# Residual products with 1024 inputs: one matmul over both halves of the input in place of two, and a second add on VectorE

## The reference

```python
# first block, twice: mixer (a state space model, then stick-breaking attention), then SwiGLU
h = layer_norm(DEEPNORM_ALPHA * h + mix, ...)                       # mix = z @ w_out, o @ w_o     1024 inputs
h = layer_norm(DEEPNORM_ALPHA * h + swiglu_ffn(h, w_gu, w_down), ...)  # w_down: 2816 inputs
# second block, twice: attention and mLSTM side by side, then an MLP
x = x + mixed @ w_out                                               # 1024 inputs
u = relu(rmsnorm(x, norm_ffn) @ w_ff1)
x = x + (u * u) @ w_ff2                                             # 4096 inputs
```

## Time and profile before

| | |
|---|---|
| median of three runs | 1340.32 us (1340.19 to 1340.81) |
| the profiled execution's own time | 1339.62 us |
| its span | 1337.7 us |
| TensorE busy | 1312.3 us (98%), 10155 matmuls |
| VectorE busy | 961.5 us (72%), 1374 instructions |
| ScalarE busy | 693.6 us (52%), 872 instructions |
| hid_both matmuls of line 430 (512 columns) | 756, 394 ns each |
| hid_both matmuls of line 420 (256 columns) | 492, 280 ns each |
| reads from HBM | 169 GB/s over the span |

### The profile page before, as it was taken

One profiled execution on the slowest core, in us unless ns is written; L12 is line 12 of the kernel. 1 busy time (PEld: TensorE's weight loads), 2 busy tenths in 40 slices (PEclk: granted clock), 3 DMA queues, 4 the chain that ended last, 5 costly groups with the idle time before them and its releaser, 6 DMA issues.

```text
span 1337.7 us, 24857 instructions
## 1 busy us (share of the span) xinstructions
PE 1312.3 (98%) x10155; PEld 1221.3 (91%) x10155; DVE 961.5 (72%) x1374; ACT 693.6 (52%) x872; POOL 56.7 (4%) x31
## 2 busy tenths in 40 slices
PE   6899999999999999999999999999999999999999
PEld 4699998889999998889989999998898999999888
DVE  8966977757865987767897687775557867877542
ACT  5874654445765654444756644444445644544332
POOL 6910000000000000000000000000000000000000
PEclk9999999999999999999999999999999999999999
DMA  8676486666443586666454546567664545556762
GB/s 158 159 189 185 133 220 188 189 189 189 154 131 105 148 219 189 188 190 189 127 158 127 182 155 200 188 189 189 189 189 127 158 127 189 190 188 188 189 189 64
DMA packets 342810, 227.82 MB, mean 170 GB/s; under 512 B 22616, under 2 KB 337792, under 8 KB 342592
## 3 DMA queue, kind: packets, MB, share of 16 engines
q1 hardware_dynamic: 341200, 226.33, 59.2%
q10 hardware_dynamic: 1520, 0.20, 0.1%
HBM read 224.40 MB, written 1.05 MB: 169 GB/s over the span
## 4 chain that ended last, share of the span: by engine, by line
PE 88%; DVE 7%; ACT 3%; DMA 1%; issue 1%; POOL 1%; SPq 0%; DVEq 0%; ACTq 0%; POOLq 0%
PE PS L430 22%; PE PS L420 15%; PE PS L421 15%; PE PS L422 15%; PE PS L431 11%; DVE w_lo L401 2%; ACT w_hi L396 1%; PE PS L1419 1%; DMA toep<-toep 1%; DVE xn L1213 1%; DVE xn L1208 1%; PE PS L2509 0%; PE PS L1403 0%; PE PS L1893 0%; DVE raw_lo L1168 0%
## 5 line engine op out<-in xcount | busy, mean ns | idle before, releaser
L401 DVE TENSOR_TENSOR w_lo<-raw,w_hi 128x2048 fp32r<-128x2048 f32 x207 | 473.3, 2289 | 132.4 <-ACT w_hi L396 131.6
L396 ACT ACTIVATE w_hi<-raw 128x2048 fp32r<-128x2048 f32 x207 | 396.5, 1916 | 199.8 <-PE PS L431 136.1
L420 PE MATMUL PS<-x_both,w_hi 128*128 128x256 f32 x1248 | 352.6, 283 | 1.0 <-DVE w_lo L401 0.5
L421 PE MATMUL PS<-x_both,w_hi 128*128 128x256 f32 x1248 | 350.8, 281 | 0.0
L422 PE MATMUL PS<-x_both,w_lo 128*128 128x256 f32 x1248 | 350.5, 281 | 0.0
L430 PE MATMUL PS<-hid_both,w_hi 128*128 128x512 f32 x756 | 264.8, 394 | 0.0
L420 PEld LDWEIGHTS PS<-x_both,w_hi 128*128 128x128 f32 x1248 | 235.5, 189 | 5.7 <-issue 2.6
L421 PEld LDWEIGHTS PS<-x_both,w_hi 128*128 128x128 f32 x1248 | 234.5, 188 | 0.1
L422 PEld LDWEIGHTS PS<-x_both,w_lo 128*128 128x128 f32 x1248 | 234.5, 188 | 0.0
L431 PE MATMUL PS<-hid_both,w_lo 128*128 128x256 f32 x756 | 211.8, 280 | 0.0
L430 PE MATMUL PS<-x_both,w_hi 128*128 128x512 f32 x544 | 189.9, 393 | 0.0
(11 more groups left out here) (405 smaller groups left out, 1607.6 us busy)
## 6 DMA issues: line engine op xcount, KB each, us to landing
raw<-in_w_ff_dram SPq DMA_DIRECT2D x128, 512.0 KB, 4.6
raw<-in_ffn_w_gu_dram SPq DMA_DIRECT2D x88, 512.0 KB, 5.0
raw<-in_w_in_dram SPq DMA_DIRECT2D x68, 512.0 KB, 4.7
raw<-in_sb_w_qkv_dram SPq DMA_DIRECT2D x24, 512.0 KB, 4.6
raw<-in_ffn_w_down_dram SPq DMA_DIRECT2D x20, 512.0 KB, 5.1
raw<-in_ssm_w_glu_dram SPq DMA_DIRECT2D x16, 512.0 KB, 6.0
raw<-in_w_out_dram SPq DMA_DIRECT2D x16, 512.0 KB, 4.2
raw<-in_ssm_w_out_dram SPq DMA_DIRECT2D x8, 512.0 KB, 4.5
```

Of the source, the lines that this page charges most:

```text
L396: nc.scalar.activation(w_hi[s][:, :], raw[s][:, :], ACT.Copy).then_inc(hi_done, 1)
L401: nc.vector.tensor_tensor(w_lo[s][:, :], raw[s][:, :], w_hi[s][:, :].bitcast(F32), ALU.subtract).then_inc(lo_done, 1)
L420: nc.tensor.matmul(dst, lhs_hi, r_hi, start=start, stop=False, skip_group_check=True)
L421: nc.tensor.matmul(dst, lhs_hi, r_lo, start=False, stop=False, skip_group_check=True)
```

## The change

`wide` now holds for output tiles 0 to 6 of every residual product, and `resid_first`, which does tiles 0 to 3 (or 0 and 1) of the four products with 1024 inputs, uses `two`. Tile 7 stays with `three`. Since `second_half` asks `wide`, VectorE adds the second half of 28 more tiles.

```diff
         def wide(g, t):
-            return g.shape == "col" and t < KT - 1
+            return t < KT - 1
...
             for kt in range(*kts):
                 pe.wait_ge(hid_done, g.in_hid + (kt // 2 if g.half else kt) + 1)
                 for m in range(2):
-                    last = three(PS[:, tile_bank(g, 2 * idx + m), 0:T], hi[:, kt, m, :], lo[:, kt, m, :], hid_hi[:, t0 + kt, :],
-                                 hid_lo[:, t0 + kt, :], kt == 0, kt == KT - 1)
+                    last = two(tile_bank(g, 2 * idx + m), hi[:, kt, m, :], lo[:, kt, m, :], hid_both[:, t0 + kt, :, :], kt == 0,
+                               kt == KT - 1)
                     if kt == KT - 1:
                         last.then_inc(chunk_done if m else tile_done, 1)
```

## The result

| | before | changed |
|---|---|---|
| median | 1340.47 us (1340.19 to 1340.81, 5 runs) | 1346.41 us (1345.70 to 1347.14, 5 runs) |
| ratio | | 1.0044, 95% interval 1.0033 to 1.0055 |
| profiled execution, its span | 1339.62 us, 1337.7 us | 1345.74 us, 1343.9 us |

A forecast was written before the change was run, and what follows sets the result against it. TensorE, busy 98%, was taken as the bound, with VectorE's lateness reaching it where slack is zero. Four products at 1.43 us make 5.7 us more, profiled time 1345.3, median 0.7 above that: 1346.0 us, range 1343.5 to 1348.2.

The forecast's parts named there:

- The pair's saving: TensorE in the four products: 0.0042 us less per pair, about 0.9 us over 224 pairs, bounds nothing and 1.5 us.
- The rival of weight loads on the path (D): TensorE's pairs come much faster, up to 26 us won, less 5.7 for waits: down to 1320; chance 2%.
- The second half: VectorE's second add on each of 28 tiles costs it 0.46 us, bounds 0.40 and 0.50.
- The other reading: From the Trainium skill: the semaphore between two VectorE adds is free, a second half costs 0.40 us, whole sum near 4.9.
- `ssm_out` and `sb_out`: VectorE's lateness, 0.05 us at `w_lo` plus 3 x 0.46 for tiles 4 to 6, delays TensorE 1.43 us each.
- `out0` and `out1`: TensorE waits for weights (0.7 us) and for the squares' mean, sharing one lateness: 1.43 us late in each product.
- VectorE's three marks: VectorE's lateness in `out0`: 0.92 us at the first `w_lo`, 1.85 at the `w_lo` for `ff1_0`, 2.10 towards the squares.
- Nothing absorbs it later: Between the four places TensorE has no other wait to give up, so the 5.7 us reach the end.
- The clock: Taken at its upper level, 2.4 GHz, throughout, with new waits of at most 1.5 us each.
- A (hidden): The adds are hidden as VectorE is only 72% busy: 0.9 us won, 1339.4, no measurable change; chance 7%.
- B (only the normed): Only the normed products pay; `out0` and `out1` swallow the delay: 2.4 us more, 1342.7; chance 8%.
- C (every add in full): Every second half counts in full: 28 x 0.46 - 0.9 = 12.0 us more, 1352.3; chance 3%.

The follow-up runs named there:

- gpsimd_wlo: The kernel before, with GpSimd making one `w_lo` in place of VectorE in each of the norms behind `ssm_out` and `sb_out`: 1343.89 us, ratio 1.0029.
- tiles_0_3: Against the kernel before, wide pairs and second adds for output tiles 0 to 3 only of the four products: 1340.56 us, ratio 1.0001.
- tiles_4_6: Against the kernel before, wide pairs and second adds for output tiles 4 to 6 only of the four products: 1344.54 us, ratio 1.0031.

## Why the prediction was right

- **The pair's saving, 0.9 us in all:** 0.9 without the second adds (0.8 by the trace), and 2.8 us for 756 pairs. Right, small as it is, and none of it reaches the end of the changed kernel. The rival of weight loads on the path (D) is excluded: pairs are 0.3486 us apart. The spacing of 131 ns for 512 columns that the prediction quoted from the Trainium skill ("TensorE: Matmul & The Clock Gate") isn't seen; the wide matmul's successor starts 0.23 us behind it.
- **The second half, 0.46 us on VectorE:** 0.46 in the trace in `ssm_out` and on the later tiles, but 0.40 on the four tiles of `out0` that stand together: they take 3.15 us where 3.3 were forecast. The other reading, that the wait between the two is free, would have given 4.9 in place of the 5.7 us that the four places show.
- **`ssm_out` and `sb_out`, 1.43 us each:** 1.39 and 1.44. The step at `w_lo` (0.05 forecast, 0.04 measured) and the 1.38 of tiles 4 to 6 (1.36) came as written. The squares' mean itself moved by 0.68, or 0.85 with the opening's 0.17 (0.82 forecast). Its wait, forecast at 0.9, shows as 0.59 us, for two reasons. The view counts from the shown end of the matmul before, behind the point where the next could start: line 898 started at 145.68, the mean would follow 0.43 later, so by the starts the wait is 0.76. And TensorE was not 0.1 sooner there but 0.09 later (145.68 against 145.76, less the opening). A wait costs some 0.1 us on top, since the stream starts up again behind it: from `shift_mean` to the next pair it is 0.35 us (132.68 to 133.03), and without the wait it was 0.24 (132.81 to 133.05). That was not in the working, and the later waits took it up.
- **`out0` and `out1`, 1.43 us each:** 1.43 and 1.46, through the two waits that share one lateness. VectorE's three marks were each forecast 0.1 too late, most of it the 0.40. The working had no wait for tile 0's bank; it took TensorE's 0.24 us, so that the wait for the weights, forecast at 0.7, is 0.41 by the starts (808.98 + 0.12 to 809.51). The sum is the same without it, because TensorE leaves when VectorE is done.
- **Nothing absorbs it later:** right. `ff1`, the long products and the next layer ran on with that lateness. It even grew, by 0.36 us in the norm behind `down0` and by 0.3 elsewhere; for that the prediction had no term. That the medians differ by 5.9 us and not by 6.4, as the traces do without the opening, is within their interval; how near the forecast came to 5.9 is in part luck.
- **The clock:** granted 0.998 over the changed kernel's span, 0.999 before. The new waits, up to 0.65 us, did nothing to it (1.00 from 146 to 150 us), nor did the one of 1.49 us in `gpsimd_wlo` (1.00 from 157 to 160).
- **Rivals:** A (hidden) and B (only the normed) fell with the waits and the halves of the change. C (every add in full) falls with `tiles_0_3`: 16 of the 28 adds cost 0.2 us.

## What to carry to other kernels

Look for the waits of the busiest engine that are only a few tenths long: there another engine's queue has zero slack, and each instruction put in front of such a place, with no idle time between, is paid in full, whatever that engine's mean share of busy time. In `ssm_out` and `sb_out` the same 0.42 us add was free on tiles 0 to 2, nearly free on tile 3, and cost its whole 0.46 on tiles 4 to 6. But the lack of such waits is no leave: `out0` and `out1` had none, and paid half of the loss, because their slack of 0.6 to 0.7 us, which only the two engines' timelines side by side show, was less than the seven adds. And before trading instructions on one engine for work on another, measure the trade per unit: here 8 pairs give TensorE 0.03 us and cost VectorE 0.46, in the long products 22 or 32 pairs give 0.09 or 0.13 and VectorE has the time.

## What was not expected

GpSimd, with an instruction that reads SBUF, holds up a VectorE instruction with two SBUF inputs for its whole length (0.68 us became 4.92), though both have separate work. And `w_lo` in the norm behind `down0` started 0.36 us later than in the kernel before, behind the same releaser, in just those four kernels that have seven more adds in front of it; `tiles_4_6` has it at a later instruction. The cause stays open.
